# The ends of the four large stages of a two-block transformer kernel: last slabs reordered, norms by tile, shared final scaling

## The reference, cut to what matters

```python
h = rms_norm(x, norm_mix) * (1 + sc1) + sh1
x = x + g1 * (mixer_1(h) @ w_out)
h = rms_norm(x, norm_ffn) * (1 + sc2) + sh2
x = x + g2 * conv_glu_ffn(h)            # up 2048 -> 11264, conv, gate, down 5632 -> 2048
x = rms_norm(x, norm_final)             # end of block 1
# block 2, the same shape with other weights and another mixer:
h = modulate(rms_norm(x, norm1), ...); x = x + gate * (mixer_2(h) @ w_out_2)
h = modulate(rms_norm(x, norm2), ...); x = x + gate * ffn_2(h)
y = rms_norm(x, norm_f)
```

## Time and profile before

| | |
|---|---|
| median of 3 runs | 2526.63 us (2525.19 to 2527.48) |
| profiled execution, span | 2525.9 us |
| PE busy | 2484.3 us (98%), 19624 matmuls |
| DVE, ACT, POOL busy | 1440.5, 1124.3, 1232.5 us |
| mean granted TensorE clock | 0.995 of full speed |
| DMA | 611.66 MB, mean 242 GB/s |
| time between a stage's last slab product and the next one's first, or the end | 9.4, 12.9, 9.3 and 18.2 us |

### The profile page before, as it was taken

One profiled execution on the slowest core, in us unless ns is written; L12 is line 12 of the kernel. 1 busy time (PEld: TensorE's weight loads), 2 busy tenths in 40 slices (PEclk: granted clock), 3 DMA queues, 4 the chain that ended last, 5 costly groups with the idle time before them and its releaser, 6 DMA issues.

```text
span 2525.9 us, 50139 instructions
## 1 busy us (share of the span) xinstructions
PE 2484.3 (98%) x19624; PEld 2273.1 (90%) x19624; DVE 1440.5 (57%) x2436; ACT 1124.3 (45%) x1324; POOL 1232.5 (49%) x500
## 2 busy tenths in 40 slices
PE   7999999999999999999999999999999999999997
PEld 5897998899999999998887877899999999998886
DVE  2536666266767767776665633265766756453433
ACT  2253334434444444454444444344544444454443
POOL 2674445675444444454443666465444444444442
PEclk8999999999999999999999999999999999999998
DMA  9974565596777777777776565386666675556553
GB/s 399 397 271 178 200 234 201 224 385 221 276 286 265 267 274 281 267 260 275 272 272 243 182 258 207 130 313 254 220 233 222 216 258 184 184 180 200 192 191 117
DMA packets 140381, 611.66 MB, mean 242 GB/s; under 512 B 15584, under 2 KB 15968, under 8 KB 115680
## 3 DMA queue, kind: packets, MB, share of 16 engines
q1 hardware_dynamic: 140256, 609.88, 66.4%
HBM read 607.72 MB, written 2.10 MB: 241 GB/s over the span
## 4 chain that ended last, share of the span: by engine, by line
issue 45%; PE 33%; POOL 21%; POOLq 1%; DVE 0%; DMA 0%; ACT 0%; DVEq 0%; SPq 0%
PE psum L1971 33%; POOL wlo L1780 21%; POOLq L1777 0%; DMA ada_raw<-adastream 0%; DVE xT L2314 0%; POOLq L1779 0%; PE psum L2204 0%; DVE psum L2314 0%; ACT arena L1794 0%; POOLq L1780 0%; ACT arena L1791 0%; DVE arena L2429 0%; DVE acc L2306 0%; DVE acc L2314 0%; DVEq L388 0%
## 5 line engine op out<-in xcount | busy, mean ns | idle before, releaser
L1780 POOL TENSOR_TENSOR wlo<-raw,whi 128x1024 fp32r<-128x1024 f32 x496 | 1232.3, 2491 | 1264.2 <-ACT whi L1791 1263.2
L1791 ACT ACTIVATE whi<-raw 128x1024 fp32r<-128x1024 f32 x760 | 800.6, 1058 | 950.1 <-PE psum L1971 716.2
L1971 PE MATMUL psum<-hi_h,whi 128*128 128x256 f32 x4224 | 1206.4, 286 | 4.6 <-DVE lo_h L2314 2.3
L1971 PE MATMUL psum<-lo_h,whi 128*128 128x256 f32 x4224 | 1190.3, 282 | 0.0
L1971 PE MATMUL psum<-hi_h,wlo 128*128 128x256 f32 x4224 | 1190.2, 282 | 0.0
L1971 PEld LDWEIGHTS psum<-hi_h,whi 128*128 128x128 f32 x4224 | 798.4, 189 | 18.7 <-issue 8.5
L1971 PEld LDWEIGHTS psum<-hi_h,wlo 128*128 128x128 f32 x4224 | 798.8, 189 | 1.7 <-issue 1.4
L1971 PEld LDWEIGHTS psum<-lo_h,whi 128*128 128x128 f32 x4224 | 798.4, 189 | 0.0
L2306 DVE TENSOR_TENSOR wlo<-raw,whi 128x1024 fp32r<-128x1024 f32 x264 | 385.1, 1463 | 268.3 <-ACT whi L1791 268.3
L2314 DVE SCALAR_TENSOR_TENSOR psum<-ada_raw,cact,psum 128x256 f32<-128x256 f32 x814 | 342.4, 483 | 24.5 <-DMA ada_raw<-adastream 21.1
L1971 PE MATMUL psum<-whi,gshi 128*128 128x512 f32 x704 | 276.0, 392 | 0.3 <-DVE wlo L2306 0.3
(11 more groups left out here) (166 smaller groups left out, 1608.8 us busy)
## 6 DMA issues: line engine op xcount, KB each, us to landing
raw<-wstream SPq DMA_DIRECT2D x760, 512.0 KB, 4.6
ada_raw<-adastream SPq DMA_DIRECT2D x168, 1024.0 KB, 6.8
arena<-adastream SPq DMA_DIRECT2D x24, 1024.0 KB, 18.0
xT<-x_in SPq DMA_DIRECT2D x8, 512.0 KB, 7.1
y_out<-xT SPq DMA_DIRECT2D x4, 512.0 KB, 2.6
gs_pages<-tabs_in SPq DMA_DIRECT2D x2, 512.0 KB, 4.2
gs_pages<-rw_in SPq DMA_DIRECT2D x2, 512.0 KB, 6.7
tabs<-tabs_in SPq DMA_DIRECT2D x1, 482.0 KB, 8.5
```

The costliest lines, as they stand in the source:

```text
L1780: nc.gpsimd.tensor_tensor(wlo[:, q, :], raw[:, q, :], whi[:, q, :].bitcast(F32), ALU.subtract).then_inc(sem.lo_ready, 1)
L1791: return nc.scalar.activation(out_, in_, ACT.Copy, scale=scale)
L1971: return nc.tensor.matmul(o, lhsT, rhs, start=start, stop=stop, skip_group_check=True)
```

## The change

- Output stages: the last two slabs of the last group are taken together and by channel block (`last_two`): each of four blocks runs through both slabs. The fourth block has a bank of its own (bank 5). DVE adds the first tiles while PE does the rest, ACT squares tile by tile, and the first two tiles' squares are summed ahead of the fourth block. The sums of the three earlier groups are moved into the last two groups.
- Down stages: the last two slabs are taken by token half, `finish` goes ahead of them; the turn of half 0 and the sums of the third group stand among the products of half 1.
- Norms: the last squares are no longer summed on 32 rows, copied and turned: PE multiplies them by a column of 1/D straight into the token column (`means`, `main_tiles`), the root adds epsilon as its bias, and ACT loads the root's table ahead of the last squares by a small operation. For N = 2 the second root and its spread come later, behind the first slabs, into bank 3.
- h is made, and waited for, tile by tile. keep_busy is left only behind the spread of the output stages (3), and is gone at N = 2.
- ACT copies two slabs of the next stage to whi ahead of the norm instead of three; the third comes behind the root.
- After N = 5 rstd is copied to SBUF; ACT multiplies ten tiles by norm_f while PE works, DVE multiplies tiles 0 to 3 and 10 to 15 and POOL tiles 4 to 9 by rstd, and six stores take the result out.
- The norm constants are folded (gain2, eps), and some semaphores are joined.

```diff
+            def store(c0, c1):
+                sp.dma_start(out[:, c0:c1, :], xT[:, c0:c1, :]).then_inc(sem.out_landed, 16)
+            sp.wait_ge(sem.y_ready, 1)
+            store(0, 4)
+            sp.wait_ge(sem.y_pool, 1)
+            store(4, 8)
+            sp.wait_ge(sem.y_ready, 2)
+            store(10, 12)
+            sp.wait_ge(sem.y_ready, 3)
+            store(12, 14)
+            sp.wait_ge(sem.y_pool, 2)
+            store(8, 10)
+            sp.wait_ge(sem.y_ready, 4)
+            store(14, 16)
+            sp.wait_ge(sem.out_landed, 96)
...
+            pool.wait_ge(sem.norm_dve, STEPS[5] + 3)
+            for c0, c1 in ((4, 8), (8, 10)):
+                nc.gpsimd.tensor_tensor(xT[:, c0:c1, :], xT[:, c0:c1, :],
+                                        rstd[:].unsqueeze(1).broadcast_to([P, c1 - c0, S]), ALU.mult
+                                        ).then_inc(sem.y_pool, 1)
...
+            def root(N, second=False):
+                act.wait_ge(sem.norm_pe, STEPS[N] + (3 if second else 1))
+                if second:
+                    ins = fn(stat[:, 2:4], bank[3][:, 0:2], ACT.Sqrt, bias=eps)
+                else:
+                    ins = fn(stat[:, 0:2], bank[6][:, 0:2], ACT.Sqrt, bias=eps2 if N == 2 else eps)
+                ins.then_inc(sem.sd_ready, 1)
+            def last_squares(N):
+                fn(stat[:, 10:11], eps, ACT.Sqrt)
+                act.wait_ge(sem.sq_used, 4 * NORMS[N] + 2)
+                for j in range(4):
+                    if j < 3:
+                        act.wait_ge(sem.x_tile, TILES_X[N] + (N in (2, 5)) + j + 1)
+                    else:
+                        act.wait_ge(sem.x_ready, 4 * N)
+                    fn(tiles(14)[:, j, :], xT[:, 12 + j, :], ACT.Square).then_inc(sem.sq_ready, 1)
+            def norm(N, n0, shift):
+                last_squares(N)
+                root(N)
+                his(n0, n0 + 3)
+                his_h = hhi if N == 2 else mhi
+                for c in range(KT):
+                    act.wait_ge(sem.u_ready, TILES_H[N] + c + 1)
+                    fn(his_h[:, c, :], norm_u(c), ACT.Identity, bias=modc[:, shift + c:shift + c + 1]).then_inc(sem.h_hi, 1)
+                    if N == 2 and c == 1:
+                        root(N, True)
+                    if c == 3 or (c >= 7 and c % 2):
+                        his(n0, n0 + (4 if c == 3 else c // 2 + 2))
+            def output(n0, N, shift):
+                for g in range(3):
                     his(n0 + g * GS + 3, n0 + (g + 1) * GS + 3)
                     if g > 0:
                         square(N, g - 1)
-                norm(N, h0, 3, n0 + 4 * GS, shift)
...
-                his(end, end + 3)
-                for tb in range(2):
-                    if tb == 0:
-                        act.wait_ge(sem.down_pe, 5 * b + 4)
-                    else:
-                        act.wait_ge(sem.slab_used, end)
-                    copy(halves(12)[:, tb, :], bank[2 + tb]).then_inc(sem.down_out, 1)
+                his(end, end + 2)
+                if b:
+                    for c in range(8):
+                        fn(xT[:, c, :], xT[:, c, :], ACT.Identity, scale=col("norm_f", c))
+                act.wait_ge(sem.down_pe, 7 * b + 4)
+                copy(halves(12)[:, 0, :], bank[2]).then_inc(sem.down_out, 1)
+                square(5 if b else 2, 2)
+                if b:
+                    act.wait_ge(sem.sq_ready, SQUARES[5] + 3)
+                    for c in range(8, 10):
+                        fn(xT[:, c, :], xT[:, c, :], ACT.Identity, scale=col("norm_f", c))
+                act.wait_ge(sem.slab_used, end)
+                for n in range(2):
+                    c = slice(n * S, (n + 1) * S)
+                    copy(halves(12)[:, 1, c], bank[3][:, c]).then_inc(sem.down_out, 1)
...
+            def last_two(n, p, N):
+                ready(n)
+                ready(n + 1)
+                for j in range(4):
+                    if j == 3:
+                        sum_tiles(N, 2)
+                    for s in range(2):
+                        q = (n + s) % RING
+                        for kk in range(2):
+                            kt = KT - 4 + 2 * s + kk
+                            w = slice(kk * 512 + j * P, kk * 512 + (j + 1) * P)
+                            ins = product(last_place(p, j), whi[:, q, w], wlo[:, q, w], mhi[:, kt, :], mlo[:, kt, :],
+                                          False, s == 1 and kk == 1)
+                        if j == 3:
+                            ins.then_inc(sem.slab_used, 1)
+                        elif s:
+                            ins.then_inc(sem.block_done, 1)
+            def slab_tok(n, p, k, first, last, kks=(0, 1), tile=None):
...
+            def sum_tiles(N, count):
+                for j in range(count):
+                    pe.wait_ge(sem.sq_ready, SQUARES[N] + 4 + j)
+                    ins = mm(bank[6][32 * j:32 * j + 32, 0:S], ones[:, 0:32], tiles(14)[:, j, :], False, True)
+                ins.then_inc(sem.sq_used, 1)
             def keep_busy(n):
                 for _ in range(n):
                     mm(bank[4 if st["spare"] == 0 else 0][:, 0:S], ident, tabs[:, 0:S], True)
-            def wide(N):
-                kinds = 4 if N == 2 else 2
-                if N < 5:
-                    keep_busy(2)
-                pe.wait_ge(sem.norm_dve, 2 * NORMS[N] - 1)
-                for n in range(kinds):
-                    ins = mm(bank[6][:, n:n + 1], ms_part[:, n * P:(n + 1) * P], tab("sel")[:, 0:1], n == 0)
-                    if n == kinds - 1:
-                        ins.then_inc(sem.norm_pe, 1)
-                if N < 5:
-                    keep_busy(3 if N == 2 else 2)
-                pe.wait_ge(sem.norm_dve, 2 * NORMS[N])
-                for n in range(kinds):
-                    ins = mm(bank[6][:, n * P:(n + 1) * P], stat[:, n:n + 1].broadcast_to([P, P]), ident, n == 0)
-                    if n == kinds - 1:
-                        ins.then_inc(sem.norm_pe, 1)
-                if N < 5:
-                    keep_busy(6)
...
+            def means(place, which, at=None, tile=None, start=False, last=False):
+                for n in range(2):
+                    lh = ms_part[:, at + n * P:at + (n + 1) * P] if tile is None else tiles(14)[:, tile, n * P:(n + 1) * P]
+                    ins = mm(place[:, n:n + 1], lh, which, start and n == 0, last)
+                return ins
+            def main_part(N):
+                pe.wait_ge(sem.norm_dve, STEPS[N] + 1)
+                at, k = (S, 0) if N == 2 else (0, 2)
+                return means(rstd_w, tab("sel")[:, k:k + 1], at, start=True)
+            def main_tiles(N, j0):
+                for j in range(j0, 4):
+                    pe.wait_ge(sem.sq_ready, SQUARES[N] + 4 + j)
+                    which = gain2[:, 12 + j:13 + j] if N == 2 else tab("sel")[:, 3:4]
+                    ins = means(rstd_w, which, tile=j, last=j == 3)
+                ins.then_inc(sem.norm_pe, 1)
+            def spread(place, c, step):
+                pe.wait_ge(sem.norm_dve, step)
+                for n in range(2):
+                    ins = mm(place[:, n * P:(n + 1) * P], stat[:, c + n:c + n + 1].broadcast_to([P, P]), ident, n == 0)
+                ins.then_inc(sem.norm_pe, 1)
             def output(n0, g0, N, x0, h_at):
-                for g in range(4):
+                for g in range(3):
                     p = (g0 + g) % 2
                     part(n0 + g * GS, p, 0, 4, h_at=h_at if g == 0 else None, h=(mhi, mlo))
-                    if g >= 2:
-                        sums(N, g - 2)
+                    if g == 2:
+                        sums(N, 0)
                     finish()
                     part(n0 + g * GS, p, 4, GS, h_at=h_at if g == 0 else None, h=(mhi, mlo))
                     st["free"][p] = (sem.x_ready, x0 + g + 1)
-                    if g < 3:
-                        finish()
+                    finish()
+                n, p = n0 + 3 * GS, (g0 + 3) % 2
+                part(n, p, 0, 2, h=(mhi, mlo), own=True)
+                sums(N, 1)
+                part(n, p, 2, 4, h=(mhi, mlo), own=True)
                 sums(N, 2)
+                finish()
+                part(n, p, 4, 6, h=(mhi, mlo), own=True)
+                last_two(n + 6, p, N)
+                st["free"][p] = (sem.x_ready, x0 + 4)
+                main_part(N)
+                main_tiles(N, 2)
                 st["spare"] = 0
-                keep_busy(5)
-                sums(N, 3)
-                wide(N)
+                spread(rstd_w, 0, STEPS[N] + 2)
+                keep_busy(3)
...
+                def last_part(tb, k, kk):
+                    q = (end - 2 + k) % RING
+                    w = slice(kk * 512, (kk + 1) * 512)
+                    t = slice(tb * P, (tb + 1) * P)
+                    rh, rl = (a[:, 1, 2 * k + kk, t] for a in (gshi, gslo))
+                    mm(bank[2 + tb], rh, whi[:, q, w], False, False)
```

(93 more changed lines are left out.)

252 lines of the change are left out of this document (112 added, 140 removed).

## The result

The changed kernel took 2535.09 us (median of 6 runs, 2533.35 to 2537.46), the kernel before 2527.06 (6 runs, 2525.19 to 2528.72): ratio 1.0033, 95% interval 1.0022 to 1.0045. It is 8 us slower. I had said 2523.5, 2518 to 2529, and given "slower" 0.06.

What follows compares the result with a forecast made beforehand. PE, busy 98% of the span, bounds the kernel; only the four stage ends could be won. Output ends 2.0 + 2.0 less 0.2 each, N = 2 0, N = 5 -0.5: 3.1 won, 2526.6 to 2523.5 us, range 2518 to 2529.

Steps and rivals of the forecast that it cites:

- Output ends: Ends of the output stages (N = 1 and 4): 2.0 us won at each, bounds 0.5 and 3.4.
- E: Moment after an output stage's last product when PE could take another; 601.33 in block 1 before the change.
- first low: First low part of h on DVE at the output ends: due at E + 4.35, ending about E + 6.1 beside POOL.
- The moved sums and the wait ahead of the fourth block: Output ends: sums moved into the product stream cost 0.6, PE's wait for tile 1's square 0.55.
- After the restart DVE needs 0.8 a tile and PE 12 x 0.12 = 1.4, so later tiles are covered: Behind the output ends: only the first tile of h would hold PE up, so no later wait was priced.
- rival (b): PE falls to 1.2 GHz at all three restarts and runs products there for long: 6 lost, 2532.6; chance 0.07.
- If the span grows, about the clock: Sign for the whole kernel: a longer span would mean the forecast was wrong about the clock; no size given.
- My other sign: If the four stretches shrink by over 10 us together, the forecast is wrong about the ports DVE and POOL share.
- The four stretches: Gaps at the four stage ends where PE does no slab product: 9.4, 9.3, 12.9 and 18.2, together 51.5 us.
- Down end of block 1: End of block 1's down stage (N = 2): result 0, with the clock falling; bounds 2.5 won, 2.0 lost.
- Last norm: Kernel's end (N = 5): 0.3 won up to the spread, 0.8 lost in the tail; 0.5 lost together.
- C: Start of a down stage's last piece, 24 products; forecast from 1367.6 in block 1 and 2502.13 at the kernel's end.

Runs made afterwards that it cites:

- The pairs: Changed kernel with h of both up stages made by DVE in pairs of tiles, as before the change: 2529.30 us, ratio 1.0010 to the kernel before.
- the late sum: Changed kernel with PE taking the ada unit's sum two slabs later in the first turn of block 1's up stage: 2530.38 us, ratio 1.0017.
- the allocation alone: Kernel before with rstd1 allocated but unused and stat at 16 columns, moving xT and arena 1056 bytes in SBUF: 2529.16 us, one run.

## Why the prediction was wrong, point by point

**Output ends: right up to the restart, wrong behind it.** I put PE's restart at E + 6.2 behind a first low blocked by POOL; it was E + 5.9, with a low of 1.60 us. The moved sums and the wait ahead of the fourth block were to cost 1.15; they cost 1.6 in each block (product 2831 to the last one takes 19.9 us and not 18.3). The two differences cancel: 1.9 won at each end up to the restart, where the sum had 2.0. The step that failed is "After the restart DVE needs 0.8 a tile and PE 12 x 0.12 = 1.4, so later tiles are covered". It holds for a tile alone (PE takes the first ten tiles without a wait), but between tiles DVE also splits slabs +3, +5, +7 and makes the ada unit, and POOL's splits block it. In the kernel before this list took 27.3 us, and PE already waited 1.7 at its end: there was no cover left. The change made the list 4.8 us longer and started it 1.3 earlier. Of the 4.8, 2.5 are the single tiles, which expose each low to ACT and to POOL: in pairs they are gone. The other 2.3 stay in pairs, and their cause is open. Against the kernel before PE lost 5.1 at the waits and 2.6 by the clock in block 1, 2.3 and 1.6 in block 2. The pairs and the late sum show it: 94.7 us with both, 103.2 without. I had read the earlier trace rows for the price of one blocked low and never added up the engine's list to the sum that PE waits for.

**The clock.** I allowed 0.2 at each output end and a fall at the down end only. It also fell behind the waits, for 6.8 and 3.4 us. In rival (b) I had the restarts as the place; seven of eleven traces of changed kernels have 3.4 or 6.8 us at half clock there in block 1, in four of them over, to 0.1 us, by the time PE restarts (605.9 to 609.3 in the trace with DVE's last scaling from PSUM). Behind it PE waits for DVE anyway: that trace has another 3.4 us from 626.3, then a shorter wait for the sum and no fall behind it, and its up stretch is 99.0, though the code is that of 103.2. In these traces half clock costs where PE is the limit and next to nothing where DVE is. Rival (b)'s 2532.6 is near the result, by another way; its mechanism isn't what the traces show. "If the span grows, about the clock" is half right: some 4.2 us of the two up turns are clock, but the waits came first. My other sign misled. The four stretches did shrink by over 10 us together (10.9), and that was to mean that I am wrong about the ports. POOL was in the way of the first low as I had said; the sign had left out what the change moves into the stream.

The Trainium skill, TensorE: Matmul & The Clock Gate, "Why this matters for your kernels", warns against idle gaps between bursts; the trace agrees in direction, 3.12 us idle at 635.65 and half clock from 638.6.

**Down end of block 1: 0 forecast, 1.1 won by the trace.** PE restarted at 1391.22, 16.9 behind the start of the last two slabs (1374.34), where I had 18.5, and the clock was at 0.50 from 1386.2 for 10.2 us, 5.2 of them behind the restart, where I had put some 3.4 without a row for it. The fall was right; its length varies from trace to trace, 6.8 to 13.7 us, which gives 157.4 to 160.5, or 2.6 won to 0.5 lost; my bounds were 2.5 won and 2.0 lost.

**Last norm: 0.5 lost forecast, 0.5 lost measured.** C is 2508.93 and the end 2533.2: 24.3 us against 23.8. The reciprocal came at C + 12.6 (12.8 forecast), the rest took 10.2 from the copy (10.2 forecast), with rows of DVE and POOL that alternate. The end-to-end agreement is partly luck: in the other unedited traces the copy of rstd starts 6.3 to 8.1 us behind the last product (7.5 here), by the clock of the one-column matmuls, so the same code would have given from 0.8 won to 1.1 lost.

**The start: not in the sum at all.** I held the first 85 us for untouched. The changed kernel is 1.8 us late at product 1200, and the allocation alone gives that.

By the two profiled traces, lost (+) or won (-): start +1.8, output end 1 with the first up turn +4.9, down end -1.1, output end 2 with its up turn +1.2, end +0.5, and between these stretches -0.1 (-0.4 by product 2880, +0.3 between the down end and output end 2): together the span's 7.3. My sum had 0, -2.0, 0, -2.0 and +0.5, and +0.4 for the clock.

## What to carry to other kernels

Before a stall is shortened, add up the list of the engine that feeds the next stage, to the last thing the bottleneck takes from it, blocked time included; if it ends level with the bottleneck, an earlier restart only moves the wait, and the cover has to be made first (order in larger pieces, consumer later). Count what is moved out of a gap into the stream as a cost: here the gaps shrank by 10.9 us and the kernel grew. A finer grain of a handover shortens the first tile and may lengthen all the others. Give new buffers a place behind the old ones, and look at the transfer rate of a load-bound stretch after any change of the layout.

## What the runs showed of the hardware

- Moving the buffers behind the new one by 1056 bytes in SBUF changed the rate of full DMA queues from 422 to 417 GB/s.
- DVE with one operand in PSUM and POOL with SBUF operands don't slow each other (DVE 0.40 a tile, POOL 3.57 for six tiles); with all operands in SBUF DVE took 0.92 a tile in the mean (2.56 and 1.48 beside POOL, 0.40 alone) and POOL 4.78. The Trainium skill, SBUF — State Buffer, "SBUF: two separate sides", has the lock for VectorE operations with two SBUF inputs, and both traces agree.
- The granted clock fell to half at the end of a single wait of 2.4 us (1776.41 to 1778.80), and in two of the three traces of the kernel before soon behind one of 1.7 us (in the second trace PE starts nothing from 633.02 to 634.75, and the clock is at half from 635.6 to 639.0; in the first the same wait brings no fall). At the ends of the stages inside the kernel and behind them it stayed there for 3.4 to 13.7 us, and at the same code it fell in some traces and not in others.
- A spare float32 matmul of 256 columns takes 0.44 us, a product in fp32r 0.12.
